# Two hybrid transformer layers on one core: the stage ahead of the experts reordered by token tile, first expert lists built on chip

## What is computed

```python
h = rms_norm(x, g_pre2) * (1.0 + sc2) + sh2
x = x + g2 * rms_norm(moe(h, lp), g_post2)

def moe(h, lp):
    t = h.reshape(B * T, D)
    scores = jax.nn.sigmoid(t @ lp['w_router'])
    sel = scores + lp['b_router']
    ...                                   # top 2 of 4 groups, by the sum of each group's two best
    _, eidx = lax.top_k(masked, TOP_K)    # 4 of 32; among equal scores the earlier expert wins
    w = jnp.take_along_axis(scores, eidx, axis=-1)
    w = w / jnp.sum(w, axis=-1, keepdims=True) * ROUTE_SCALE
    combine = jnp.sum(jax.nn.one_hot(eidx, N_EXPERTS) * w[..., None], axis=1)
    gu = jnp.einsum('nd,edf->nef', t, lp['w_exp_gu'])
    a = jax.nn.silu(gu[..., :256]) * gu[..., 256:]
    a = (a * combine[..., None]).reshape(-1, 32 * 256)
    routed = a @ lp['w_exp_down'].reshape(32 * 256, D)
    sgu = t @ lp['w_sh_gu']
    shared = (jax.nn.silu(sgu[:, :256]) * sgu[:, 256:]) @ lp['w_sh_down']
    return routed + shared
```

## Time and profile before

| | us |
|---|---|
| three timed runs | 2178.5, 2179.73, 2184.72 |
| median | 2179.73 |
| the profiled execution | 2174.03 |
| its span | 2172.2 |
| TensorE busy in the span | 1867.6 (86%) |
| TensorE weight loads | 1391.7 (64%) |
| VectorE busy | 1300.6 (60%) |
| ScalarE busy | 1036.5 (48%) |
| GpSimd busy | 498.1 (23%) |

### The profile page before, as it was taken

The page is one execution under the profiler, slowest core; times in us unless marked ns, Lnnn a source line. Parts: engine busy times, 40 slices in busy tenths (PEclk is TensorE's granted clock), DMA queues, the critical chain, the costliest instruction groups (busy, mean ns, idle before and its releaser), DMA issues. The chain is left out here.

```text
span 2172.2 us, 27171 instructions
## 1 busy us (share of the span) xinstructions
PE 1867.6 (86%) x9234; PEld 1391.7 (64%) x9234; DVE 1300.6 (60%) x1857; ACT 1036.5 (48%) x1709; POOL 498.1 (23%) x430
## 2 busy tenths in 40 slices
PE   4999898999977699899649989989999767999992
PEld 2987566788864466666448866668887635666661
DVE  2244566634445578888753455665444475888885
ACT  2332247433332477777533423573333424877781
POOL 0002410400000445454100042114000022454540
PEclk8999899999998799999869999989999888999996
DMA  7543472233324399999834335403333336999994
GB/s 255 166 135 120 149 247 103 92 117 117 133 89 176 113 340 349 342 342 341 295 94 153 118 112 185 147 16 116 125 127 126 118 117 214 347 349 354 351 326 175
DMA packets 145062, 417.82 MB, mean 192 GB/s; under 512 B 26160, under 2 KB 36688, under 8 KB 118864
## 3 DMA queue, kind: packets, MB, share of 16 engines
q1 hardware_dynamic: 124208, 376.54, 50.0%
q0 software_dynamic: 17952, 33.74, 4.8%
q10 hardware_dynamic: 2816, 6.39, 0.8%
HBM read 409.70 MB, written 32.15 MB: 203 GB/s over the span
## 5 line engine op out<-in xcount | busy, mean ns | idle before, releaser
L1596 DVE TENSOR_TENSOR W_split<-W,W_split 128x2048 fp32r<-128x2048 f32 (+2 forms) x92 | 215.1, 2340 | 425.7 <-ACT W_split L1224 425.7
L2106 PE MATMUL psum<-W_split,qT_split 128*128 128x512 f32 (+3 forms) x1536 | 412.8, 381 | 15.9 <-PEq L2402 8.0
L1224 ACT ACTIVATE W_split<-W 128x2048 fp32r<-128x2048 f32 (+2 forms) x92 | 170.0, 1854 | 386.0 <-PE psum L2106 386.0
L2106 PEld LDWEIGHTS psum<-W_split,qT_split 128*128 128x128 f32 x1536 | 286.0, 191 | 71.4 <-issue 16.4
L2106 PE MATMUL psum<-W_split,scratch_split 128*128 128x512 f32 x864 | 280.5, 396 | 0.4 <-DVE hT_split L1591 0.4
L2106 PE MATMUL psum<-W_split,hT_split 128*128 128x512 f32 x576 | 213.7, 398 | 5.8 <-DVE scratch_split L1791 5.8
L2349 PE MATMUL psum<-W_split,zf_split 128*96 128x512 f32 x512 | 202.9, 396 | 0.0
L2106 PEld LDWEIGHTS psum<-W_split,scratch_split 128*128 128x128 f32 x864 | 162.2, 189 | 39.1 <-DVE hT_split L1591 0.6
L2106 PE MATMUL psum<-W_split,kT_split 128*128 128x512 f32 (+3 forms) x480 | 178.5, 372 | 0.0
L2106 PEld LDWEIGHTS psum<-W_split,hT_split 128*128 128x128 f32 x576 | 109.1, 190 | 31.6 <-DVE scratch_split L1791 6.3
L1146 POOL COPY vm<-vm 96x1 uint32 x64 | 64.4, 1006 | 242.7 <-ACT zf L1497 242.7
(11 more groups left out here) (341 smaller groups left out, 3940.2 us busy)
## 6 DMA issues: line engine op xcount, KB each, us to landing
W<-in_w_exp_gu SPq DMA_DIRECT2D x128, 1024.0 KB, 8.1
W<-in_w_exp_down SPq DMA_DIRECT2D x64, 1024.0 KB, 8.8
W<-in_w_in SPq DMA_DIRECT2D x60, 1024.0 KB, 5.1
W<-in_w_mod SPq DMA_DIRECT2D x40, 1024.0 KB, 5.3
W<-in_w_br SPq DMA_DIRECT2D x16, 1024.0 KB, 5.0
zf<-y_rows SPq DMA_DIRECT2D x12, 1024.0 KB, 6.9
W<-in_w_out SPq DMA_DIRECT2D x8, 1024.0 KB, 5.0
W<-in_w_mod SPq DMA_DIRECT2D x3, 2048.0 KB, 18.9
```

What stands on the lines that cost most here:

```text
L1224: nc.scalar.activation(high(j), piece(SPLITS[j]), ACT.Copy).then_inc(S["high_ready"], 1)
L1596: V.tensor_tensor(piece(SPLITS[j], Wr), piece(SPLITS[j]), high(j).bitcast(F32), ALU.subtract).then_inc(S["low_ready"], 1)
L2106: ins = nc.tensor.matmul(bank(job, piece_size(key)[1]), act_part[:, k0 + k, t * P:(t + 1) * P], w_part[:, k, :], start=first and (k, i) == ...
```

## The change

The middle stage goes by token tile; the choice of experts is computed by another formula; the rows of experts 0 to 3 are gathered by lists that are built on the chip, without the table in DRAM; and in the expert loop silu and product stand ahead of the second gate-up half. Indentation is shortened in the diffs, and a line of three dots stands for lines left out.

The plan: the jobs of the first turns are per row tile, half emptied by ScalarE and half by VectorE; the router's job follows them; the place job and a new job `first` come ahead of most of the shared expert; banks are given by hand.

```diff
-    for k in range(KD):
-        jobs.add(("h2", k), "act")
+    for t in range(T):
+        jobs.add(("h2", t, 0), "act", 2 * t)
+        jobs.add(("h2", t, 1), "dve", 2 * t + 1)
+    jobs.add(("route",), "act", 6)
...
+            jobs.add(("hrow", t, c), "act", 2 * t + c)
+    jobs.add(("place",), "act", 6)
+    jobs.add(("gu", "s", 0), "dve", 7)
+    jobs.add(("first",), "dve", 5)
...
+        jobs.add(("y", "s", t, 0), "dve", (3, 6, 3)[t])
+        jobs.add(("y", "s", t, 1), "act", (4, 7, 4)[t])
```

```diff
-    pe.wait_ge(S["mixture_rows"], T)
-    for k in range(KD):
...
+    turn_normed(0)
+    turn_normed(1)
+    bank_free(("route",))
+    route(0)
+    turn_normed(2)
+    route(1)
+    route(2).then_inc(S["psum_filled"], 1)
...
+    gate_up_shared(0, 0, KD // 2)
     pe.wait_ge(S["chosen_ready"], 1)
     pe.wait_ge(S["ones_ready"], 1)
...
+    gate_up_shared(0, KD // 2, KD).then_inc(S["psum_filled"], 1)
+    pe.wait_ge(S["at_place"], 1)
+    bank_free(("first",))
+    for e in range(4):
+        ins = multiply(psum[0:CAP, J.bank(("first",)), 2 * e:2 * e + 2], [(at_place[:, t, e, :], tokens[:, t, :]) for t in range(T)])
+    ins.then_inc(S["psum_filled"], 1)
+    for t in (1, 2):
+        bank_free(("gu", "s", t))
+        gate_up_shared(t, 0, KD).then_inc(S["psum_filled"], 1)
...
+    turn_shared(0)
+    for t in range(T):
+        if t < T - 1:
+            turn_shared(t + 1)
+        down_shared(t)
+        if t != 1:
+            pe.wait_ge(S[f"x_landed{t // 2}"], 16)
```

```diff
+    dve.wait_ge(S["mod_gain"], 1)
+    modulate_rows(0)
     pre_norm(T - 1)
-    for t in range(T):
-        empty(("hrow", t, 0), dealt(t, 0), bank(("hrow", t, 0)).rearrange("p (q k) -> p q k", k=KD))
...
-    rank(rt[:, R_MSEL], rt[:, R_TOP, :, 0:TOPK], rt[:, R_RANK], NE)
...
+    above, same, nth, chosen = rt[:, R_RANK], rt[:, R_TMP], rt[:, R_POS], rt[:, R_TOP]
+    V.tensor_tensor(above, rt[:, R_MSEL], least, ALU.is_gt)
+    link(V.tensor_tensor(same, rt[:, R_MSEL], least, ALU.is_equal))
+    V.tensor_reduce(mu[:, 0:3], above, AX, ALU.add)
+    link(V.tensor_tensor_scan(flat(R_POS), flat(R_SLOT), flat(R_TMP), 0.0, ALU.mult, ALU.add))
+    link(V.tensor_tensor(nth, nth, mu[:, 0:3, None].to_broadcast([P, T, NE]), ALU.add))
+    link(V.scalar_tensor_tensor(same, nth, float(TOPK), same, ALU.is_le, ALU.mult))
...
+    link(V.tensor_tensor(pos_first, counts[:, 0:T, 0:4], chosen[:, :, 0:4], ALU.mult))
+    V.tensor_tensor(at_place, pos_first[:, :, :, None].to_broadcast([P, T, 4, CAP]),
+                    places[:, None, None, :].to_broadcast([P, T, 4, CAP]), ALU.is_equal).then_inc(S["at_place"], 1)
...
+    product_shared(0)
+    dve.wait_ge(*filled(("first",)))
+    V.tensor_scalar(first_f[0:CAP], bank(("first",), 8, slice(0, CAP)), float(NO_TOKEN), None, ALU.add).then_inc(S["dve_emptied"], 1)
+    dve.wait_ge(*emptied(("first",)))
+    V.tensor_copy(first_u[0:CAP], first_f[0:CAP]).then_inc(S["first_ready"], 1)
+    of_choices(slot, slot_f)
+    V.tensor_copy(slot_u, slot_f).then_inc(S["slots_ready"], 1)
+    product_shared(1)
...
                 gu_low(e, 0, tile * 2 + 5)
+            if not (last and e == 1):
+                product(BANK_GU + 1 - e, 1 - e, tile + T + 2)
+            if not last:
                 gu_low(e, 1, tile * 2 + 6)
             if not (last and e == 1):
-                product(BANK_GU + 1 - e, 1 - e, tile + T + 2)
                 dn_low(1 - e, tile * 2 + 5)
```

```diff
+    silu_shared(0)
     for h in range(2):
         gu_high(0, h, 16)
+    silu_shared(1)
     act.wait_ge(S["cache_out"], 16 * 8)
     dn_high(0, 16)
...
             if not last:
                 gu_high(e, 0, turn * 16 + 32 + 16 * e)
-                gu_high(e, 1, turn * 16 + 32 + 16 * e)
             if not (last and e == 1):
                 act.wait_ge(*job_filled(turn, e, "gu", 2 if last else 0))
                 nc.scalar.activation(silu[0:CAP, 1 - e, :], psum[0:CAP, BANK_GU + 1 - e, 0:FF], ACT.Silu).then_inc(S["silu_ready"], 1)
+            if not last:
+                gu_high(e, 1, turn * 16 + 32 + 16 * e)
```

```diff
     load_down(0, expert("w_exp_down", 0))
+    for t in range(T):
+        sp.wait_ge(*emptied(("hrow", t, 1)))
+        sp.dma_start(a["token_rows"][t * P:(t + 1) * P, :], xn2[:, t, :]).then_inc(S["rows_out"], 16)
     sp.wait_ge(*filled(("gu", "s", T - 1)))
     load_gate_up(1, expert("w_exp_gu", 1))
```

```diff
+    pool.wait_ge(S["x_cleared"], 1)
+    pool.wait_ge(S["rows_out"], 16 * T)
+    pool.wait_ge(S["first_ready"], 1)
+    for e in range(2):
+        gather_first(e, e)
     pool.wait_ge(S["table_reset"], 16)
     pool.wait_ge(S["slots_ready"], 1)
     for i in range(T * TOPK):
...
-    nc.gpsimd.memset(xg[0:CAP], 0.0).then_inc(S["x_cleared"], 1)
-    pool.wait_ge(S["slots_out"], 16 * T * TOPK)
...
+        gather_first(2 + e, e)
+        if e == 0:
+            pool.wait_ge(S["slots_out"], 16 * T * TOPK)
```

More of the change, by code:

```diff
@@ L41 @@
 EG = NE // NG
+NO_TOKEN = 1 << 16
 ROUTE_SCALE = 2.5
@@ L113, in constants @@
         lam[layer] = [init, 1.0 - init]
-    return k, np.ascontiguousarray(earlier.astype(np.float32)), lam
+    return k, route, lam
 class PsumJobs:
@@ L520, in trunk @@
         iota = const[:, K_IOTA:K_IOTA + NE]
-        earlier = vm[:, 0:RANK_COLS]
-        before = earlier.rearrange("p (i j) -> p i j", i=NE)
+        route_consts = vm[:, 0:ROUTE_COLS]
+        before = vm[:, R_EARLIER:R_EARLIER + NG * NG].rearrange("p (i j) -> p i j", i=NG)
+        places = vm[:, R_PLACE:R_PLACE + CAP]
+        tokens = vm[:, R_TOKEN:R_TOKEN + 2 * T].rearrange("p (t w) -> p t w", w=2)
         rt = Pb[:, :].rearrange("p (s t e) -> p s t e", s=12, t=T)
@@ L1961, in _ @@
                     V.tensor_copy(turns_u, turns_f).then_inc(S["tables_ready"], 1)
-                    for t in range(T):
-                        for c in range(2):
-                            empty(("y", "s", t, c), acc[:, t, c * C:(c + 1) * C], bank(("y", "s", t, c)))
                     dve.wait_ge(S["tables_ready"], 1)
```

268 lines of the change are left out of this document (152 added, 116 removed).

## The result

The changed kernel takes 2108.1 us (median of four runs, 2104.4 to 2111.9), the kernel before 2179.1: a ratio of 0.967 with a 95% interval of 0.9645 to 0.9695. Five more runs on another occasion gave 2105.5 and a ratio of 0.9668 (0.9645 to 0.9692). The gain is 71 us where 73.2 had been summed, and the time lies in the range of 2088 to 2122. That the sum came this close is partly luck: errors of opposite signs cancel in it, once inside the middle stage and once between the loop and its start.

The account below looks back on a forecast made before the run. TensorE's chain was taken to bound the middle stage, DMA loads the expert loop. Middle stages 63.8, loop's start 5.4 and loop 4 sum to 73.2 us: 2100.8 from the profile, 2106.5 from the median, forecast 2104, range 2088 to 2122.

Parts of the forecast that it names:

- The way to the router: Layer 1's middle stage: turns and modulation by row tile end the router at 1725.0 instead of 1735.97, 11 us gone.
- The second rival: TensorE keeps the lower clock through turns back and first gate-up tile, 2.3 us more a layer: 2114; chance 0.10.
- TensorE's own work behind the router: Layer 1, router to first expert product: if no engine is late, TensorE's work alone sets the end, 45.6 us.
- Choosing: VectorE's choice after ranking shrinks from 11.6 to 2.0 us; TensorE doesn't wait for it, with 1 us of cover.
- The first lists: Lists built on chip let the first gathers precede the scatters; gathered rows land some 8 us ahead of their turn.
- The loop's start: First two expert products run at 5.57 us instead of 6.93, TensorE coming from work: 5.4 us in two layers.
- The loop: Expert loop: silu and product ahead of the second weight half give 0 to 12 us, taken as 4; DMA limits.
- The rule weighed: VectorE instructions with two SBUF inputs may hold up GpSimd's scatters; by the rows alone the sum stays at 2104.
- scatters late: Rival: GpSimd's scatters delayed beside VectorE, up to 25 us with ten free; 2104 to 2134, likeliest 2109; chance 0.13.
- lists late: Rival: first lists don't come early, TensorE waits for gathered rows; 2118, or 2136 behind scatters and table; chance 0.06.
- a loop freed in full: Rival: expert loop was held by its order, not DMA; 44 us come back instead of 4: 2064; chance 0.05.
- a slower loop: Rival: in the expert loop the second weight half is converted and subtracted too late; up to 2216; chance 0.03.

Follow-up runs that it names:

- The fillers: Changed kernel plus filler products on TensorE, 8 and 3 of 512 columns, while it waits for the first two normalised row tiles: 2097.8 us, ratio 0.9625.

## Why the prediction was right, step by step

**The middle stage** was to give 63.8 us in the two layers and gave 64.2, with two errors in it that cancel; the numbers that follow are layer 1's. *The way to the router* was forecast at 18.5 us from the output projection's end and took 22.0. The start of the chain was right (first turn at +4.3, first router product at +10.0); the failed term is "one router tile is a third of 7.17, 2.4", which measured 3.5 at the lower level. VectorE's modulation, taken at 0.25 an operation without a row, took 0.34. The second rival had named the low clock, but placed it at the turns back and the gate-up, and held against it that TensorE has no pauses by then. The rows show it from the first turn to the end of the turns back, without a pause from the router's first product on. The fillers showed that it is the limit, and its price: 9 us, 4.5 and 4.0 in the two middle stages. *TensorE's own work behind the router* was forecast at 45.6 and took 42.4: gate-up, count and lists 24.7 instead of 26.2 (the gate-up had been priced with a slow start), turns, down products and gathered rows 12.8 instead of 14.9.

**Choosing**: 7.4 forecast from the router's last product to the choice, 7.2 measured; 1 us of cover forecast, 1.15 measured. That a later choice is paid in full was confirmed, and the lower clock behind the wait adds 4 us or more in each layer.

**The first lists** came 4 us later than forecast behind the output projection, and their rows landed 12.7 us ahead of their turn instead of 8. The twelve products took 2.0, not 2.7.

**The loop's start** (5.4 for the full clock) was wrong: it gave nothing. The first product did take 5.7 instead of 6.93, but then TensorE stood for 3.28, where it had stood for 2.13, because the product of silu and up now waits on VectorE behind expert 1's subtractions and row parts (1741.31 to 1746.65), which were done by then in the kernel before. The second product took 7.1, in the kernel before 6.9. From the start of the first to the end of the second, layer 1 gained 0.3 and layer 0 lost 1.6. The failed sentence is "now it comes from work": the work ends with the first product.

**The loop** was sized at 4 and is worth 8 to 9. The step that failed is the view it rested on: a stretch of 100 us in the loop's middle, where loads set the pace. The first four tiles behind the second run from loaded weights, TensorE sets the pace there, and the order gives back its whole wait, 4 us in each layer. By the prediction's own sign, a tile below 9.7, its view of the loop fails for these tiles, at 9.2, and holds for the rest, at 10.2. In the profiled pair only the first layer's 4.0 shows in the loop's length; in the second profile the loops are 2.3 and 4.3 shorter than before, so the lengths alone don't show in which layer it stays. So 63.8 + 5.4 + 4 became 64 + 0 + 8 to 9, near the same total by luck.

**The rule weighed**: the scatters beside VectorE's subtractions took 2.44 and 2.22 where the others took 1.0, and when they were moved the long ones were again those beside subtractions of the gate-up weights. The Trainium skill, page "SBUF — State Buffer", section "Who interferes with whom", says that a VectorE instruction with two SBUF inputs shuts out a GpSimd one that reads SBUF; the rows agree in which scatters are long, though the subtractions of the down weights (1.17 each) held up the scatters beside them by 0.3 us at most in this profile. The twelve scatters took 18.2 and 19.1 us in the two layers, where they took 15.2 before: 3 and 4 us, not the 25 of the rival, and 7 to 8 are free.

**The other rivals**: scatters late had ten free where there are 7 to 8; lists late was priced at 16 a layer and measured 13 to 14; a loop freed in full and a slower loop did not come: TensorE's waits for the gate-up's subtractions are 1.8 us in the whole run.

## What to carry to other kernels

Work that is moved ahead can land in a stretch where the engine's clock is down: the router overtook 5 us of turns and came 1.1 us earlier. Read the granted clock of the stretch into which work is moved, not that from which it comes. A wait of TensorE can cost more than its length, 13 us for one of 9, since the work behind it began at the lower level; constant products that fill unavoidable waits were worth 9 us here. Of a loop bound by loads, read the first tiles apart: there the order of the engines still counts.

## What the hardware showed that was not expected

- TensorE, busy for 7.00 of 7.00 us with products of 32 columns and turns, was granted 0.50 throughout. Two executions of the same rows in one program, with the same waits ahead to 0.01 us, got different levels (6.87 and 3.66 for the same 32 router products).
- Behind the wait of 11.2 for gathered rows TensorE was granted 0.50 for the turns and the first down products, and the down products took 9.02 instead of 7.03. The Trainium skill, page "TensorE: Matmul & The Clock Gate", section "HAM oscillation — how this bites in real kernels", says that work behind a long DMA wait starts at the lower clock; this wait agrees with it.
- The level also fell shortly behind short waits, 5.38 instead of 3.68 behind one of 1.13 and 7.44 instead of 5.44 for the router behind one of 2.06, and without any wait, 5.36 instead of 2.82 for the turns back. So it is not shown that the short waits caused it.
- What decides between the levels stays open: the fillers show that work in the waits can keep the clock up, not how much of it is needed.
